# The time mix with two recurrences side by side, one set-up step behind both in each round, and the bonus values kept in DRAM

## The reference, cut to what matters

```python
def step(state, inp):                       # per head, t = 0..511
    r_t, w_t, k_t, v_t, a_t, b_t = inp
    sa = jnp.einsum('bhvk,bhk->bhv', state, a_t)
    state = (state * w_t[:, :, None, :]
             + sa[..., None] * b_t[:, :, None, :]
             + v_t[..., None] * k_t[:, :, None, :])
    y_t = jnp.einsum('bhvk,bhk->bhv', state, r_t)
    return state, y_t
...
y = (y - mean) * rsqrt(var + GN_EPS) * ln_w + ln_b      # per head
bonus = jnp.sum(r_h * k_h * r_k, -1, keepdims=True) * v_h
return ((y + bonus) * g) @ w_o
```

## Time and profile before

| engine | busy us | share of the span |
|---|---|---|
| PE (TensorE matmul) | 2191.7 | 87% |
| DVE | 1136.3 | 45% |
| ACT | 903.6 | 36% |
| POOL | 166.0 | 7% |

### The profile page before, as it was taken

One profiled execution on the slowest core, in us unless ns is written; L12 is line 12 of the kernel. 1 busy time (PEld: TensorE's weight loads), 2 busy tenths in 40 slices (PEclk: granted clock), 3 DMA queues, 4 the chain that ended last, 5 costly groups with the idle time before them and its releaser, 6 DMA issues. The chain is left out here.

```text
span 2519.9 us, 32530 instructions
## 1 busy us (share of the span) xinstructions
PE 2191.7 (87%) x13786; PEld 1596.5 (63%) x13786; DVE 1136.3 (45%) x1732; ACT 903.6 (36%) x1430; POOL 166.0 (7%) x175
## 2 busy tenths in 40 slices
PE   8999999976999777899999989976987988888884
PEld 7778888855766665588888867765876333333331
DVE  4447555348466454576554342746555111111112
ACT  5335333237663333454432244634323211111110
POOL 0000000000001120000000000000420111111010
PEclk9889999988999887899999999976998989989897
DMA  5112222222220101132222323121205999999995
GB/s 206 67 67 101 100 100 75 100 86 90 77 76 13 21 15 52 66 110 84 100 90 92 102 92 104 65 67 21 57 12 212 382 419 418 412 405 405 394 409 225
DMA packets 107542, 377.27 MB, mean 150 GB/s; under 512 B 55008, under 2 KB 55792, under 8 KB 68736
## 3 DMA queue, kind: packets, MB, share of 16 engines
q1 hardware_dynamic: 85264, 294.34, 31.6%
q10 hardware_dynamic: 9744, 69.21, 6.6%
q0 software_dynamic: 12384, 11.58, 1.6%
HBM read 375.31 MB, written 27.53 MB: 160 GB/s over the span
## 5 line engine op out<-in xcount | busy, mean ns | idle before, releaser
L599 PE MATMUL ps<-xh,wh 128*128 128x512 f32 x1224 | 487.0, 398 | 51.7 <-DVE wl L563 30.8
L600 PE MATMUL ps<-xl,wh 128*128 128x512 f32 x1224 | 482.7, 394 | 0.0
L601 PE MATMUL ps<-xh,wl 128*128 128x512 f32 x1224 | 481.6, 393 | 0.0
L563 DVE TENSOR_TENSOR wl<-raw,wh 128x2048 fp32r<-128x2048 f32 (+2 forms) x123 | 254.9, 2072 | 249.3 <-ACT wh L557 249.3
L3645 PE MATMUL ps<-egu,XT 128*64 128x512 f32 x1088 | 273.9, 661 | 82.3 <-DMA egu<-e_up 76.8
L599 PEld LDWEIGHTS ps<-xh,wh 128*128 128x128 f32 x1224 | 233.4, 191 | 112.6 <-DVE wl L563 37.3
L601 PEld LDWEIGHTS ps<-xh,wl 128*128 128x128 f32 x1224 | 233.4, 191 | 49.7
L600 PEld LDWEIGHTS ps<-xl,wh 128*128 128x128 f32 x1224 | 233.7, 191 | 49.1 <-issue 0.7
L557 ACT ACTIVATE wh<-raw 128x2048 fp32r<-128x2048 f32 (+2 forms) x123 | 212.8, 1731 | 99.3 <-PE ps L1082 70.6
L3645 PEld LDWEIGHTS ps<-egu,XT 128*64 128x64 f32 x1088 | 93.9, 151 | 238.7 <-issue 222.5
L3663 DVE TENSOR_TENSOR HIDT<-ps,SIL 128x256 f32<-128x256 f32 x34 | 14.4, 424 | 349.7 <-ACT SIL L3655 349.7
(11 more groups left out here) (557 smaller groups left out, 3335.1 us busy)
## 6 DMA issues: line engine op xcount, KB each, us to landing
egu<-e_gate SPq DMA_DIRECT2D x68, 1024.0 KB, 14.1
egu<-e_up SPq DMA_DIRECT2D x68, 1024.0 KB, 24.8
ed<-e_down ACTq DMA_DIRECT2D x64, 1024.0 KB, 11.1
raw<-up SPq DMA_DIRECT2D x44, 1024.0 KB, 4.9
raw<-down SPq DMA_DIRECT2D x32, 704.0 KB, 4.0
raw<-rwkv_kr SPq DMA_DIRECT2D x8, 1024.0 KB, 4.8
raw<-in_dn SPq DMA_DIRECT2D x8, 1024.0 KB, 4.9
raw<-sgu_v SPq DMA_DIRECT2D x4, 1024.0 KB, 10.3
```

The source lines that it names most:

```text
L563: e.tensor_tensor(K.WL[s][:, 0:n], K.RAW[r][:, 0:n], K.WH[s][:, 0:n].bitcast(F32), SUB).then_inc(*K.w_low.mark(i))
L599: e.matmul(o, h[:, q, k], x_high[:, k], start=k == 0, stop=False)
L600: e.matmul(o, h[:, q, k], x_low[:, k], start=False, stop=False)
L601: last = e.matmul(o, l[:, q, k], x_high[:, k], start=False, stop=k == KT - 1)
```

## The change

The four groups are set up in two pairs. The order is now: all eight product steps of front 0, the turning of the values, the rest of front 0, front 1 beside the gate, back 0 (with row solve 1 woven in on DVE). Then a loop takes, in each round, one step of recurrence 0 (later 2), one of recurrence 1 (later 3), and one of a third stretch: back 1, front 2, front 3, eight empty steps, back 2, back 3, and three output groups of two tiles each. A recurrence starts when the back of its group has been issued, recurrences 2 and 3 also only behind 0 and 1; an output group starts when the recurrence of its two tiles has been issued. The last two tiles follow after the loop, as before.

Each chain has its own ST, RH and VU, and two PSUM banks: a in the first columns of both, u and s in the first bank, y in the second. The state's part of the output is issued behind u, and the wait for ACT's copy of y stands ahead of a. VU holds one chunk, so the next chunk's values are copied behind the copy of y. TT, TN and RKB have a place for each group; MT has one for all. The inverse and its transpose lie side by side in SBUF and come back in eight transfers of twice the size. SP sends and fetches in the order of pairs. LW goes to DRAM behind the projection and comes back in three parts behind recurrence 1, since its place is needed. The row solve yields at eight points in place of four.

The core of the diff; addresses of tiles, semaphores and renamed arguments are left out:

```diff
-            self.items.append((src, n, kind, (i + (i >= self.first["rwkv_o"])) % 2, None if kind == "raw" else ns % 2))
+            self.items.append((src, n, kind, i % 2, None if kind == "raw" else ns % 2))
...
+def diagonal_out_sp(K, e, q):
...
     for r, p, c in SPOTS:
-        e.dma_start(md[16 * r:16 * r + 16].rearrange("a (i j) -> i a j", i=16), MT[p, 0:16, c])...
+        e.dma_start(md.rearrange("(a r) (i j) -> r i a j", r=8, i=16)[r], K.MT[p, 0:16, c])...
     e.wait_ge(*K.diag_out(name, 7))
...
     e.dma_start(FB[:, :, :].rearrange("p i j -> p (i j)"), md)...
+
+def inverse_in_sp(K, e, q):
     e.wait_ge(*K.dve_diag(name, "both"))
-    e.dma_start(xd, X[:, :, :, :].rearrange("p z i j -> p (z i j)"))...
+    for z in range(2):
+        half = z if q % 2 else 1 - z
+        e.dma_start(inv[16 * half:16 * half + 16].rearrange("a r i j -> (a r) (i j)"), X[:, z]...)...
...
     for r, p, c in SPOTS:
-        for z, dst in enumerate((TT, K.TN)):
-            src = xd[16 * r:16 * r + 16, 256 * z:256 * z + 256].rearrange("a (i j) -> i a j", i=16)
-            e.dma_start(dst[p, 0:16, c], src)...
+        e.dma_start(both[p, :, c], inv[:, r].rearrange("a i j -> i a j"))...
...
 def front_act(K, e, q):
-    if q > 1:
-        e.wait_ge(*K.diag_out(f"rw{q - 2}", 7))
-        e.wait_ge(*K.pool_solve(q - 2, "masked", 1, 5))
+    if q:
+        e.wait_ge(*K.diag_out(f"rw{q - 1}", 7))
+        e.wait_ge(*K.pool_solve(q - 1, "masked", 1, 5))
...
+ROWS_STOPS = (4, 7, 9, 11, 12, 13, 14, 15)
-        if n in (5, 8, 11, 13):
+        if n in ROWS_STOPS:
             yield
...
 def recur_pe(K, e, q):
+    z, A, Y = set_of(K, q), 2 * (q % 2), 2 * (q % 2) + 1
...
         e.wait_ge(*(K.dve_recur(q, "st", ch - 1) if ch else K.dve_recur(q, "zero")))
+        if ch:
+            e.wait_ge(*K.act_recur(q, "y", ch - 1))
...                                                     # a, yield, u, then the state's part of y
+class Course:
+    def until(self, *steps):
+        while not self.passed.issuperset(steps):
+            yield
+    def then(self, stretch, step):
+        yield from stretch
+        self.passed.add(step)
+        yield
+
+def three_abreast(first, second, beside):
+    left = [first, second, beside]
+    while left:
+        for g in list(left):
+            ...                                         # one step of each in turn
+
+def core(C, recur, beside):
+    def two(q):
+        yield from C.until(("solved", q))
+        yield from C.then(C.counted(recur(q), q), ("recurred", q))
+        yield from C.until(("solved", q + 2))
+        yield from C.then(C.counted(recur(q + 2), q + 2), ("recurred", q + 2))
+    three_abreast(two(0), two(1), beside)
...
-EARLY_GROUPS = (range(0, 3), range(3, 6))
+EARLY_GROUPS = (range(0, 2), range(2, 4), range(4, 6))
...
 def rwkv_sp(K, e):
-    for q in range(4):
-        solve_sp(K, e, q)
+    e.wait_ge(*K.dve_scale(KT - 1, "bv"))
+    e.dma_start(K.lws, K.LW[:, :, :])...
+    diagonal_out_sp(K, e, 0)
+    diagonal_out_sp(K, e, 1)
+    inverse_in_sp(K, e, 0)
+    inverse_in_sp(K, e, 1)
+    ...                                                 # the same for 2 and 3
+    e.wait_ge(*K.solve_sum(3, 5, 1, "TT"))
+    load_weights(K, e, K.first["rwkv_o"], K.first["rwkv_o"] + 1)
+    e.wait_ge(*K.recur_sum(1, 7, "y"))
+    for i, to in enumerate((K.LWA, K.LWB, K.LWC)):
+        e.dma_start(to[:, :], K.lws[:, 2 * i + 2 * (i > 0):2 * i + 4])...
...
 def rwkv_pe(K, e):
-    for q in range(3):
-        weave([recur_pe(K, e, q), chain(front_pe(K, e, q + 2) if q < 2 else nothing(12), back_pe(K, e, q + 1))], 2)
-    weave([recur_pe(K, e, 3), chain(group_pe(K, e, EARLY_GROUPS[0]), nothing(4), group_pe(K, e, EARLY_GROUPS[1]))], 2)
+    def beside():
+        yield from C.then(back_pe(K, e, 1), ("solved", 1))
+        yield from chain(front_pe(K, e, 2), front_pe(K, e, 3), nothing(SOLVE_GAP))      # SOLVE_GAP = 8
+        yield from C.then(back_pe(K, e, 2), ("solved", 2))
+        yield from C.then(back_pe(K, e, 3), ("solved", 3))
+        for i, js in enumerate(EARLY_GROUPS):
+            yield from C.until(("recurred", i))
+            yield from chain(group_pe(K, e, js), nothing(2))
+    core(C, lambda q: recur_pe(K, e, q), beside())
...
 def rwkv_dve(K, e):
-    weave([back_dve(K, e, 0)], 1)
+    weave([back_dve(K, e, 0), rows_dve(K, e, 1)], 2)
...
+        yield from chain(front_dve(K, e, 2), abreast(front_dve(K, e, 3), chain(nothing(3), rows_dve(K, e, 2))), nothing(SOLVE_GAP))
+        yield from C.then(abreast(back_dve(K, e, 2), rows_dve(K, e, 3)), ("solved", 2))
```

More of the change, by code:

```diff
@@ L1615, in set_of @@
 def set_of(K, q):
[L1616 removed]
+    return K.sets[q]
 def head_items(v):
@@ L1831, in back_pe @@
                 for h in (0, 64):
-                    last = e.matmul(o[h:h + 64, a], M[h:h + 64, a], K.TN[h:h + 64, 8 * i + a], start=True, stop=True)
+                    last = e.matmul(o[h:h + 64, a], M[h:h + 64, a], K.TN[q][h:h + 64, 8 * i + a], start=True, stop=True)
             last.then_inc(*K.solve_sum.mark(q, l, i, "Z"))
@@ L1892, in abreast @@
             yield
+SOLVE_GAP = 8
 def recur_pe(K, e, q):
-    z = set_of(K, q)
-    K.board.point("PE", "recur", q)
-    for t in K.board.all_at("recur", q):
-        e.wait_ge(*t)
+    z, A, Y = set_of(K, q), 2 * (q % 2), 2 * (q % 2) + 1
+    ST, RH, VU = K.ST[q % 2], K.RH[q % 2], K.VU[q % 2]
+    if q < 2:
+        for t in K.board.emptied(("low", 12 + A)) + K.board.emptied(("low", 12 + Y)):
+            e.wait_ge(*t)
+    else:
+        e.wait_ge(*K.dve_recur(q - 2, "sum", 7))
+        e.wait_ge(*K.act_recur(q - 2, "y", 7))
     e.wait_ge(*K.dve_solve(q, 5, 1, "TT"))
@@ L1909, in recur_pe @@
         e.wait_ge(*(K.dve_recur(q, "st", ch - 1) if ch else K.dve_recur(q, "zero")))
-        for jl in range(2):
-            for par in range(2):
-                r = slice(64 * par, 64 * par + 64)
-                last = e.matmul(K.ps[P_, par, 64 * jl:64 * jl + 64], K.AR[r, 0, 2 * q + jl, f:f + 64], K.ST[r, jl], start=True, stop=True)
-        last.then_inc(*K.recur_sum.mark(q, ch, "a"))
         if ch:
@@ L1926, in recur_pe @@
                 hl = 2 * jl + par
-                last = e.matmul(K.ps[P_, 2, 128 * par + 64 * jl:128 * par + 64 * jl + 64], z["TT"][P_, 4 * hl + n], K.RH[P_, par, jl],
+                last = e.matmul(K.ps[P_, A, 128 + 128 * par + 64 * jl:192 + 128 * par + 64 * jl], z["TT"][P_, 4 * hl + n], RH[P_, par, jl],
                                 start=True, stop=True)
         last.then_inc(*K.recur_sum.mark(q, ch, "u"))
+        for jl in range(2):
+            for par in range(2):
+                r = slice(64 * par, 64 * par + 64)
+                e.matmul(K.ps[r, Y, 128 + 64 * jl:192 + 64 * jl], ST[r, jl], K.AR[r, 1, 2 * q + jl, f:f + 64], start=jl == 0, stop=False,
+                         skip_group_check=True)
         yield
@@ L2044, in group_pe @@
     yield
-    for _ in range(4 if w == 3 else 5):
-        yield
+    yield from nothing(4)
 def group_act(K, e, js):
@@ L2201, in rwkv_pe @@
     first = front_pe(K, e, 0)
-    for _ in range(4):
+    for _ in range(8):
         next(first)
@@ L2225, in rwkv_act, with beside @@
     weave([back_act(K, e, 0)], 1)
-    for q in range(3):
-        weave([recur_act(K, e, q), chain(front_act(K, e, q + 2) if q < 2 else nothing(12), back_act(K, e, q + 1))], 2)
-    weave([recur_act(K, e, 3), chain(group_act(K, e, EARLY_GROUPS[0]), output_rows_act(K, e, EARLY_GROUPS[0]),
-                                     output_weights_act(K, e), group_act(K, e, EARLY_GROUPS[1]),
-                                     output_rows_act(K, e, EARLY_GROUPS[1]))], 2)
+    C = Course()
+    C.passed.add(("solved", 0))
+    def beside():
+        yield from C.then(back_act(K, e, 1), ("solved", 1))
+        yield from chain(front_act(K, e, 2), front_act(K, e, 3), nothing(SOLVE_GAP))
+        yield from C.then(back_act(K, e, 2), ("solved", 2))
+        yield from C.then(back_act(K, e, 3), ("solved", 3))
+        for i, js in enumerate(EARLY_GROUPS):
+            yield from C.until(("recurred", i))
+            if i == 2:
+                yield from output_weights_act(K, e)
+            yield from chain(group_act(K, e, js), output_rows_act(K, e, js))
+    core(C, lambda q: recur_act(K, e, q), beside())
     K.board.point("ACT", "rwkv")
@@ L2255, in rwkv_dve, with beside @@
     weave([second, rows_dve(K, e, 0)], 2)
[L2256 to L2262 removed]
+    weave([back_dve(K, e, 0), rows_dve(K, e, 1)], 2)
+    C = Course()
+    C.passed.add(("solved", 0))
+    def beside():
+        yield from C.then(back_dve(K, e, 1), ("solved", 1))
+        yield from chain(front_dve(K, e, 2), abreast(front_dve(K, e, 3), chain(nothing(3), rows_dve(K, e, 2))), nothing(SOLVE_GAP))
+        yield from C.then(abreast(back_dve(K, e, 2), rows_dve(K, e, 3)), ("solved", 2))
+        yield from C.then(back_dve(K, e, 3), ("solved", 3))
+        for i, js in enumerate(EARLY_GROUPS):
+            yield from C.until(("recurred", i))
+            if i == 2:
```

(5 more changed lines are left out.)

218 lines of the change are left out of this document (125 added, 93 removed).

## The result

The changed kernel takes 2523.0 us (median) against 2513.6 of the kernel before, a ratio of 1.0032 with the interval 1.0020 to 1.0043: 9.4 us more, where 4.1 more were forecast.

A forecast was written before the change was run, and what follows sets the result against it. In the time mix PE bound back steps, elsewhere it waited for DVE's state update or ran at a low clock. Start +7.5 and stage -3.4 (202.1 against 205.5) gave +4.1 us, 2517 on the median; 2497 to 2538 at 8 in 10.

The forecast's parts named there:

- start: From group 1's last MT copy to recurrence 0: later inverses, row solve 1 in back 0, clock: +7.5 us (3 to 10).
- (e): Wait for inverses 2, which leave only when row solve 2 ends in pass 37; PE idles: 8.5 us.
- (f): Back 2 alone, row solve 3 woven in, cold start: 11.2 + 2.3 + 0.5 = 14 us.
- (b): Back 1 with four chunks of a recurrence beside it: 17.6 + 1 us for the clock.
- (c): Front 2 with four chunks of either chain beside it: 27 us (24 to 35).
- (h): Back 3 with four chunks of chain 2: 19 us, taken from the 19.1 measured before.
- (d): Front 3 with four chunks of chain 1 and row solve 2: 28 us (24 to 34.3).
- (i): Output group 0 beside both chains, passes 71 to 82: 26 us (21 to 30).
- (j): Output group 1 beside one chain: 23 us (19 to 26).
- Rival (3): Clock stays at 1.2 GHz through front 2 and output group 0: 17 us more, +21, 2534 us; chance 0.12.
- rival (2): Inverse trips cheaper, 6.5 us each: 19.5 instead of 24.5, start 5.5 instead of 7.5; -2.9, 2510 us; chance 0.15.
- rival (1): Two chains fill each other's waits, clock stays at 2.4 GHz: 15.5 us less, -11.4, 2502 us; chance 0.26.

The follow-up runs named there:

- both edits: Changed kernel with row solves 1 and 3 wholly ahead of the back adds on DVE, and group 0's inverses sent ahead of FB: 2496.9 us, 0.9930 of the kernel before.

## Why the prediction was right in kind and short in size

The forecast gave a small loss made of trips and a third group against what two chains share. Step by step, forecast and measured (us):

```
start 7.5 / 9.15          (e) wait, inverses 2    8.5 / 9.3
(a) wait, inverses 1 8 / 8.5        (f) back 2 alone      14 / 16.2
(b) back 1 + chain 18.6 / 20.7      (g) wait, inverses 3   8 / 7.4
(c) front 2 + chains 27 / 26.3      (h) back 3 + chain    19 / 21.2
(d) front 3 + solve 28 / 24.8       (i) (j) (k) groups    71 / 70.6
sum (a) to (k) 202.1 / 205.0, before 205.5
```

**The step that failed is the size of the clock's cost behind the idle waits.** The mechanism was named, the terms for it were too small. The prediction's words were "17.6 + 1 for the clock" in (b), 0.5 for a cold start in (f) and 1 in the start. (h) was 19.1 us taken over from the earlier trace rows, a row at 0.91 where the 17.6 of (b) had 1.00, so some 1.5 of clock stood in it unsaid. That makes 3 us for (b), (f) and (h); held at 1.00 they took 51.2 us instead of 58.1, so the clock cost 6.9. This is 3.9 of the 6.5 us that the three came out over the forecast. The rest is that backs 1 and 3 beside a chain took 18.8 us even at 1.00, where 17.6 was the row before; no run shows why. The forecast had the fact before it: the back at 0.91 in the earlier trace rows stands behind the stretch at 0.55. It took that row for (h) and gave less to (b), (f) and the start, whose waits are longer. Rival (3) put the low clock into the wrong place: it feared (c) and (i), which came out at 26.3 and 25.9 us, at 0.94 and 0.79.

**Luck.** The forecast missed by 5.3 us and not by more because (d) was 3.2 too long. With (d) as measured its sum would have been +0.9.

**The start.** The first matmul of back 0 came at 820.01, 826.4 with the offset, where 826.5 was forecast. SP's timeline is as worked out, group 1's sends and FB ahead of group 0's inverses, eight fetches in 4.0 us:

```profile
803.84 3.74 SPq L1650 DMA_DIRECT2D rw1md<-MT  x8
810.67 0.34 SPq L1657 DMA_DIRECT2D rw1FB<-rw1md  x1
811.05 0.92 SPq L1666 DMA_DIRECT2D rw0inv<-rw0X  x2
813.56 4.02 SPq L1670 DMA_DIRECT2D TT3TNTT<-rw0inv  x8
```

The whole error of the start is in back 0, 16.2 us against 14.5, at the 0.74 shown above. Back 2, the same step with a row solve woven in, took 13.6 at 1.00, so by that the clock cost back 0 about 2.6 where 1 was given (an estimate; no run holds the clock up in this kernel's back 0).

**The waits** came to 25.2 us against 24.5 (8.5, 9.3 and 7.4), which settles rival (2): it wanted 19.5. They were seen as the price of the change; that two of the three hung on the place of a row solve on DVE, and could go by moving it, was not seen.

**The fronts.** (c) was right, (d) 3.2 us too long: its solve took 4.4 + 3.6 us, as assumed, with none of POOL's masks beside it, and the clock stayed at 0.86. The 2.5 us that the forecast took for POOL's share there was row solve 1's; solve 2's products had taken 6.4 us before, so its share was 2.0. What made (d) shorter than forecast is not shown. Together they took 51.1, below the 52 to 60 named as a sign of being right and just at the point where rival (1) would have had the change break even. PE's waits for the state update did shrink as that rival has it; but (d) has one chain, and the pairing in (c) was worth about 1 us, so the rival's reason, chains that fill each other's waits, is not what did it.

**Costed at nothing.** The bonus came back in time: DVE did not wait for LWA. The first product's wait for ACT's copy of y, 8.9 us in three waits, is 3.8 and 4.6 us behind ACT's table loads, Ln and Exp in (i) and (j), which held the copy of u before; the sum of the groups came out at the forecast. Since the last part of the stretch differs by 8.4 us between executions, about as much as that wait, this does not show that the wait cost nothing.

**POOL and DVE.** In back 0 the last product of row solve 1 met POOL's masks, which begin at 832.29, and took 1.48 us; the same product of solve 0, while POOL only zeroed a tile, took 0.56:

```profile
805.52 0.95 POOL L1692 MEMSET TT1TNTT<- 128x1024 f32 x1
...
805.55 0.56 DVE L1824 TENSOR_TENSOR rw0PR<-rw0FB,rw0X 128x225 f32<-128x225 f32 x1
...
832.29 5.39 POOL L1700 TENSOR_TENSOR tmp<-MT,cst 128x512 f32<-128x512 f32 x4 [24.92 <-PE ps L1857]
...
832.47 1.48 DVE L1824 TENSOR_TENSOR rw1PR<-rw1FB,rw1X 128x225 f32<-128x225 f32 x1
```

That agrees with the rule of the Trainium skill, SBUF — State Buffer, section Who interferes with whom, that a VectorE operation with two SBUF inputs and a GpSimd operation reading SBUF exclude each other. The loss of about 1 us that the prediction set beside its sum was there, in solve 3 as well.

## What to carry to other kernels

A wait that empties PE for some 7 to 9 us cost here its length and then some: the dense work behind it started at the lower clock, 1.9 to 2.6 us for each of three back steps. Before a recurrence is doubled, look at what its set-up hangs on: a solve that ends with the step before it puts its whole trip through DRAM on the path, and moving it ahead on an engine that is idle there was worth some 20 us, where the pairing of the first two chains was worth about 1 at most. An early start of work on an engine that has other work due only moved the wait here.

## What the runs showed of the hardware

Behind waits of 6 us and more the clock in the next 13 to 21 us was 0.74 to 0.90, and 1.00 in back 0 of the kernel before, behind 2.3. It is not the last wait alone: in the kernel before, back 3 ran at 0.91 behind 2.0 us, with the stretch at 0.55 ahead of it. Nor does the step ahead decide it: with both edits back 0 ran at 0.83 to 0.84 in three kernels, and back 1 behind it at 0.85 in one and at 1.00 in the two others. In the one PE had been busy for 0.45 of the 2.6 us ahead of back 1, in the others for 0.45 of 1.5 and 1.6. The steps of a lone chain in the wait, small products with gaps between them, ran at 0.68 and left back 1 at 0.88; products end to end in the same wait left it at 1.00. Where it settles between these no run shows. The Trainium skill, TensorE: Matmul & The Clock Gate, section What's actually happening, says that "the default state is throttled, and activity releases the throttle"; these rows agree with it. Eight fetches of 256 KB in all took 4.0 us to issue (4.95 in group 1), the sixteen of half the size 8.5: the pitch on SP's queue, 0.5 us, went by the transfer, not by its bytes.
